# Attention of the first mixer: weighing by rounded and low parts instead of fp32 products, and one product for the two squares

## The reference

```python
proj = u @ w_in[l]
qk_raw, v, o_pre, gates, glu = jnp.split(proj, ...)
qk = jax.nn.silu(causal_dwconv(qk_raw, qk_conv_w[l], qk_conv_b[l]))
h = mlstm_chunkwise(heads(q), heads(k), heads(v), gates_i, gates_f)
h = rms_norm(h, ml_norm_g[l]) * jax.nn.sigmoid(o_pre)
y = causal_dwconv(a * jax.nn.sigmoid(gt), cv_dw_w[l], cv_dw_b[l])
y = jax.nn.silu(layer_norm(y, cv_ln_g[l], cv_ln_b[l]))
mix = jnp.concatenate([h, y], axis=-1) @ w_out[l]
```

## Time and profile before

| | us |
|---|---|
| median of 3 runs | 2322.71 |
| lowest and highest | 2318.79, 2326.07 |
| the profiled execution | 2319.68 |
| its span | 2317.9 |
| PE busy | 2218.1 (96%) |
| DVE busy | 1135.3 (49%) |
| ACT busy | 641.2 (28%) |
| POOL busy | 1481.5 (64%) |

### The profile page before, as it was taken

One profiled execution on the slowest core, in us unless ns is written; L12 is line 12 of the kernel. 1 busy time (PEld: TensorE's weight loads), 2 busy tenths in 40 slices (PEclk: granted clock), 3 DMA queues, 4 the chain that ended last, 5 costly groups with the idle time before them and its releaser, 6 DMA issues.

```text
span 2317.9 us, 27215 instructions
## 1 busy us (share of the span) xinstructions
PE 2218.1 (96%) x9696; PEld 1737.0 (75%) x9696; DVE 1135.3 (49%) x1971; ACT 641.2 (28%) x1108; POOL 1481.5 (64%) x710
## 2 busy tenths in 40 slices
PE   7999999999999998899999999997999989999997
PEld 4777776767888886788777888885777767888886
DVE  5778878884343104666543222006777844222101
ACT  2222323322222103444342111003555534111100
POOL 3756654566777887454278777887232238877785
PEclk9999999999999999999999999998999999999999
DMA  5322323642233332222123323331212212223232
GB/s 224 101 79 83 93 82 100 231 151 91 90 96 94 100 100 90 65 73 74 46 73 104 95 90 98 102 100 64 64 55 65 63 55 82 91 90 99 91 108 83
DMA packets 56513, 216.48 MB, mean 93 GB/s; under 512 B 6232, under 2 KB 6232, under 8 KB 53232
## 3 DMA queue, kind: packets, MB, share of 16 engines
q1 hardware_dynamic: 52992, 206.96, 27.6%
q10 hardware_dynamic: 3440, 8.44, 1.1%
HBM read 213.23 MB, written 2.15 MB: 93 GB/s over the span
## 4 chain that ended last, share of the span: by engine, by line
PE 56%; issue 22%; POOL 16%; DVE 4%; ACT 2%; POOLq 0%
PE ps L336 51%; POOL w_hi L868 8%; POOL w_lo L874 8%; PE ps L538 2%; ACT u_hi L420 1%; DVE u_lo L468 1%; DVE ps L485 1%; PE ps L1201 1%; PE ps L1233 1%; POOL acc L459 0%; PE ps L1208 0%; DVE ps L479 0%; PE ps L1247 0%; PE ps L375 0%; DVE ho L2190 0%
## 5 line engine op out<-in xcount | busy, mean ns | idle before, releaser
L868 POOL TENSOR_TENSOR w_hi<-raw,ones 128x1024 fp32r<-128x1024 f32 x315 | 602.0, 1911 | 595.3 <-DMA raw<-in_wstream 594.7
L874 POOL TENSOR_TENSOR w_lo<-raw,w_hi 128x1024 fp32r<-128x1024 f32 x342 | 837.7, 2449 | 194.6 <-ACT w_hi L1602 169.9
L336 PE MATMUL ps<-u_hi,w_hi 128*128 128x512 f32 x1760 | 719.0, 409 | 11.1 <-POOL w_lo L874 5.6
L336 PE MATMUL ps<-u_lo,w_hi 128*128 128x512 f32 x1760 | 698.5, 397 | 0.0
L336 PE MATMUL ps<-u_hi,w_lo 128*128 128x512 f32 x1760 | 698.0, 397 | 0.0
L336 PEld LDWEIGHTS ps<-u_hi,w_hi 128*128 128x128 f32 x1760 | 333.5, 190 | 89.5 <-issue 7.7
L336 PEld LDWEIGHTS ps<-u_hi,w_lo 128*128 128x128 f32 x1760 | 332.1, 189 | 81.6
L336 PEld LDWEIGHTS ps<-u_lo,w_hi 128*128 128x128 f32 x1760 | 333.2, 189 | 75.9 <-issue 3.1
L336 PE MATMUL ps<-f_hi,w_hi 128*128 128x512 f32 x528 | 208.6, 395 | 0.0
L336 PE MATMUL ps<-f_lo,w_hi 128*128 128x512 f32 x528 | 208.6, 395 | 0.0
L336 PE MATMUL ps<-f_hi,w_lo 128*128 128x512 f32 x528 | 208.6, 395 | 0.0
(11 more groups left out here) (328 smaller groups left out, 2894.8 us busy)
## 6 DMA issues: line engine op xcount, KB each, us to landing
raw<-in_wstream SPq DMA_DIRECT2D x342, 512.0 KB, 3.5
ada_buf<-in_ada SPq DMA_DIRECT2D x16, 1024.0 KB, 6.8
ada_start<-in_ada SPq DMA_DIRECT2D x8, 1024.0 KB, 16.7
cbc<-decay_rows ACTq DMA_DIRECT2D x8, 512.0 KB, 3.6
x<-in_xT SPq DMA_DIRECT2D x1, 2048.0 KB, 8.0
bc<-gate_rows ACTq DMA_DIRECT2D x4, 512.0 KB, 5.0
out_T<-x ACTq DMA_DIRECT2D x8, 256.0 KB, 2.2
prm<-in_params SPq DMA_DIRECT2D x1, 357.5 KB, 2.9
```

The lines of the kernel that those rows point to most:

```text
L336: last = nc.tensor.matmul(out, a, b, start=(start and k == 0 and i == 0), stop=(stop and k == nk - 1 and i == 2))
L868: g.tensor_tensor(w_hi[slot][:], raw[slot][:], ones[:, 0:1].to_broadcast([P, D]), ALU.mult).then_inc(chunk_hi, 1)
L874: g.tensor_tensor(w_lo[slot][:], raw[slot][:], w_hi[slot][:].bitcast(f32), ALU.subtract).then_inc(chunk_split, 1)
```

## The change

- The turned values and the product of scores and decays are held as a rounded part (`vt_hi`, `sp_hi`) and a low part (`vt_lo`, `sp_lo`). The numerators are three float32r products per block, the denominator two, with a float32r tile of ones (`ones_r`), which POOL fills at the start.
- ACT writes `vt_hi` where it wrote `vt`, and rounds `sp` (`att_high_act`: at the top of the next head, ahead of its first gate sigmoid; behind the last head ahead of the rounded heads). DVE forms `vt_lo` from banks 6 and 7 (`att_values_low_dve`, steps vl0, vl1, at the top of the next head ahead of the scores' product) and `sp_lo` (`att_low_dve`, step spl, behind it).
- PE waits in the scores for vl0 and vl1 instead of ACT's copies, and ahead of the denominator for spl instead of sp3.
- `vt_lo` lies on `vf`, `sp_hi` on `wt`, `sp_lo` on `sp`. So ACT writes `vf` and `wt` of the next head only when the numerators are done (num1).
- DVE adds the two squared numerators (`att_sum_dve`, step sum; after ten taps of the next head, and behind the divisor for the last one), and PE multiplies the sum with ones once.

```diff
@@ places
-    vt = place("vt", 2 * T, shape=[2, NT, P])
+    vt_lo = nc.alloc_sbuf_tensor_at("vt_lo", [P, 2, NT, P], f32r, offset=v_at)
+    vt_hi = place("vt_hi", 2 * T, f32r, [2, NT, P])
+    sp_hi = nc.alloc_sbuf_tensor_at("sp_hi", [P, 1280], f32r, offset=wt_at)
+    sp_lo = nc.alloc_sbuf_tensor_at("sp_lo", [P, 1280], f32r, offset=here[0])
@@ GpSimd
+        g.memset(ones_r[:].bitcast(f32), 1.0).then_inc(const_ready, 1)
@@ PE
                 if st in (1, 2):
-                    pe.wait_ge(a_v.sem, a_v.at(f"vt{st - 1}", h))
+                    pe.wait_ge(v_att.sem, v_att.at(f"vl{st - 1}", h))
...
-            pe.wait_ge(v_att.sem, v_att.at(f"sp{NT - 1}", h))
+            pe.wait_ge(v_att.sem, v_att.at("spl", h))
             for st in range(NT):
-                last = nc.tensor.matmul(ps[b][:, st * P:T], ones[:] if w is None else vt[:, w, st, :],
-                                        sp[:, WOFF[st]:WOFF[st] + T - st * P], start=(st == 0), stop=(st == NT - 1))
+                hi, lo = [t[:, WOFF[st]:WOFF[st] + T - st * P] for t in (sp_hi, sp_lo)]
+                if w is None:
+                    pairs = [(ones_r[:], hi), (ones_r[:], lo)]
+                else:
+                    pairs = tri(vt_hi[:, w, st, :], vt_lo[:, w, st, :], hi, lo)
+                last = matmuls(ps[b][:, st * P:T], pairs, start=(st == 0), stop=(st == NT - 1))
...
-            pe.wait_ge(v_att.sem, v_att.at("dn", h))
-            for e in range(2):
-                pe.wait_ge(a_n.sem, a_n.at(f"n{e}", h))
-                last = nc.tensor.matmul(ps[3][:], ones[:], sq[e][:], start=(e == 0), stop=(e == 1))
-            p_att.did(last, "hs")
+            pe.wait_ge(v_att.sem, v_att.at("sum", h))
+            p_att.did(nc.tensor.matmul(ps[3][:], ones[:], sq[0][:], start=True, stop=True), "hs")
@@ ACT
             if h:
-                act.wait_ge(v_att.sem, v_att.at(f"sp{NT - 1}", h - 1))
+                act.wait_ge(p_att.sem, p_att.at("num1", h - 1))
...
+        def att_high_act(h):
+            act.wait_ge(v_att.sem, v_att.at(f"sp{NT - 1}", h))
+            a_n.did(A(sp_hi[:], sp[:], ACT.Identity), "sph")
...
         for h in range(H1):
+            if h:
+                att_high_act(h - 1)
             gate_act(h, 0)
...
                 if h and e == 0:
-                    act.wait_ge(p_att.sem, p_att.at("vt1", h - 1))
+                    act.wait_ge(p_att.sem, p_att.at("num1", h - 1))
...
+        att_high_act(H1 - 1)
         act.wait_ge(gemm_done, C_WOUT1)
@@ DVE
+        def att_values_low_dve(h):
+            for e in range(2):
+                dve.wait_ge(a_v.sem, a_v.at(f"vt{e}", h))
+                v_att.did(V.tensor_tensor(vt_lo[:, e, :, :], ps[6 + e][:].rearrange("p (s c) -> p s c", c=P),
+                                          vt_hi[:, e, :, :].bitcast(f32), ALU.subtract), f"vl{e}")
...
+        def att_low_dve(h):
+            dve.wait_ge(a_n.sem, a_n.at("sph", h))
+            v_att.did(V.tensor_tensor(sp_lo[:], sp[:], sp_hi[:].bitcast(f32), ALU.subtract), "spl")
+        def att_sum_dve(h):
+            dve.wait_ge(a_n.sem, a_n.at("n1", h))
+            v_att.did(V.tensor_tensor(sq[0][:], sq[0][:], sq[1][:], ALU.add), "sum")
...
             if h:
+                att_values_low_dve(h - 1)
                 att_scores_dve(h - 1)
+                att_low_dve(h - 1)
                 att_divisor_dve(h - 1)
             gated(h, 0)
-            conv_taps(h, 0, 29, 16)
+            conv_taps(h, 0, 29, 20)
+            if h:
+                att_sum_dve(h - 1)
+            conv_taps(h, 0, 19, 16)
...
+        att_values_low_dve(H1 - 1)
         dve.wait_ge(p_ln.sem, p_ln.at("mu"))
         for n in range(KT):
             v_ln.did(V.tensor_tensor(y[:, n, :], y[:, n, :], ps[4][:], ALU.subtract), f"yc{n}")
         att_scores_dve(H1 - 1)
+        att_low_dve(H1 - 1)
...
         att_divisor_dve(H1 - 1)
+        att_sum_dve(H1 - 1)
         att_variance_dve(H1 - 1)
```

More of the change, by code:

```diff
@@ L126, in build @@
     ones = place("ones", P)
+    ones_r = place("ones_r", P, f32r)
     mean_w = place("mean_w", P)
@@ L701, in build @@
     v_dg = Steps(ctx, nc, "diag_dve", ["diag"])
-    v_att = Steps(ctx, nc, "att_dve", [f"sp{i}" for i in range(NT)] + ["dm", "dn", "d2", "vr", "h0", "h1", "hg0", "hg1"])
+    v_att = Steps(ctx, nc, "att_dve", ["vl0", "vl1"] + [f"sp{i}" for i in range(NT)] + ["spl", "dm", "dn", "d2", "sum", "vr", "h0", "h1", "hg0", "hg1"])
     a_sg = Steps(ctx, nc, "gate_sig_act", ["sg0", "sg1"])
@@ L709, in build @@
     a_wt = Steps(ctx, nc, "decay_act", [f"dg{i}" for i in range(NT)] + [f"off{i}" for i in range(NT - 1)])
-    a_n = Steps(ctx, nc, "att_act", ["n0", "n1", "ln", "rstd"])
+    a_n = Steps(ctx, nc, "att_act", ["sph", "n0", "n1", "ln", "rstd"])
     p_att = Steps(ctx, nc, "att_pe", ["vt0", "vt1", "qk0", "qk1", "qk2", "qk3", "den", "num0", "num1", "hs"])
@@ L849, in _ @@
         g.memset(eps_col[:, 1:2], 1e-37).then_inc(const_ready, 1)
-        pool.wait_ge(const_ready, 9)
+        pool.wait_ge(const_ready, 10)
         for t in (ident, ident_b):
@@ L909, in _ @@
     def _(pe):
-        pe.wait_ge(const_ready, 16)
+        pe.wait_ge(const_ready, 17)
         pe.wait_ge(v_set.sem, v_set.at("lv71"))
@@ L1294, in _ @@
         a_set.did(A(cvec[:], prm[:, COL["c"]:COL["c"] + KT], ACT.Sigmoid), "sig_c")
-        act.wait_ge(const_ready, 16)
+        act.wait_ge(const_ready, 17)
         norm_act(act, norms[0], None, lambda n: mod[:, n:n + 1])
@@ L1395, in _ @@
                         act.wait_ge(p_att.sem, p_att.at(f"vt{e_}", h))
-                        a_v.did(A(vt[:, e_, :, :], ps[6 + e_][:], ACT.Identity), f"vt{e_}")
+                        a_v.did(A(vt_hi[:, e_, :, :], ps[6 + e_][:], ACT.Identity), f"vt{e_}")
         for n in range(KT):
@@ L1676, in _ @@
         v_set.did(V.tensor_tensor(cvec[:], cvec[:], prm[:, COL["c"]:COL["c"] + KT], ALU.mult), "c")
-        dve.wait_ge(const_ready, 16)
+        dve.wait_ge(const_ready, 17)
         v_set.did(V.tensor_tensor(number[2], number[0], number[1], ALU.bitwise_xor), "xor")
```

## The result

| | before | after |
|---|---|---|
| median, us | 2321.32 (4 runs) | 2338.36 (4 runs, 2336.25 to 2344.44) |
| the profiled execution, us | 2319.68 | 2338.52 |
| its span, us | 2317.9 | 2336.7 |

The account below looks back on a forecast made before the run. It took PE as the bound, matmuls busy 96% of the span. Stalls 12.2 + clock 6.0 - products 6.0 + end 6.7 = +18.9 us, from 2319.68 to 2338.6, as a median 2341.6, range 2330 to 2352.

Parts of the forecast that it names:

- The stalls: PE waits in scores block 1 for DVE's vl0: 5.7, 3.1 and 3.4 us after heads 0 to 2, sum 12.2.
- The clock: PE's clock falls behind each stall, costing 2.0 us (0 to 2.9) each: +6.0 us for three stalls.
- The rival without a fall: PE's clock does not fall behind the stalls: +10.9 us, 2333.6; chance 0.17.
- The products: Fewer PE passes in numerators, denominator and squares: 2.0 us saved per head, 6.0 for three heads.
- The three heads together: Stalls 12.2, clock +6.0 and products -6.0 over the three heads between gemms: 12.2 us.
- The end of the stage: Behind the last head: stall 3.1, clock 2.0, rounding 1.2, d2 and sum 1.3, one product less 0.86: +6.7 us.
- Costs put at nothing: Between heads, rounding and low part of sp, sum of squares, moved reuse waits; at the start, the memset: hidden or free.
- the margin of 2.3 us: In each head, sp's chain takes 4.7 us after the scores; PE reaches the denominator after 7.0, so no wait.
- The contention rival: Low part of sp on DVE slowed beside POOL to 6.9 us, about 3.1 us per head: 2350.9; chance 0.10.
- The covered wait: DVE reads the banks before PE ends scores block 0, so no stall: -4.4 us, 2318.3; chance 0.08.

Follow-up runs that it names:

- The experiment with the wait alone: Kernel before, fp32 products unchanged, plus DVE's two subtractions at the change's place, results unused, with the scores waiting for them: 2344.74 us, ratio 1.0098.
- the first experiment: The changed kernel with DVE's low parts of the values moved before the last eight taps of the same head: 2322.11 us, ratio 1.0001.
- the reordering: The first experiment's kernel with another order of DVE's and ACT's steps behind the last head: 2321.68 us, ratio 0.9987 to the kernel before.
- the experiment with the later scores: The changed kernel with the scores four weight tiles later in PE's gemm, DVE's order untouched: 2329.64 us, ratio 1.0032 to the kernel before.
- the last experiment: The reordering's kernel without DVE's running sum of the last convolution tile; PE forms the mean in two products: 2314.55 us, ratio 0.9959 to the kernel before.
- the last two experiments: The reordering (2321.68 us) and the same kernel with the last running sum moved from DVE to PE (2314.55 us).

## Why the prediction was right

- **The stalls** came where and by what they were said to come. Behind the last head the release was forecast 6.7 us after the scores' start (378.91 - 372.20) and came at 6.9 (389.14 - 382.23). In the heads 12.2 us were forecast and 9.34 measured, and nearly all of the difference is in the first: 5.7 forecast, 3.10 found. There PE reached the scores 2.1 us later than before, held up by DVE already in the queries and keys (the 2.5 us for qk in the view of waits), while the release was at 139.77, forecast 140.10. That the release came so near is luck: DVE began its running sum 1.8 us later than before (138.42 against 136.66), but found POOL done and took 0.69 us for it instead of 2.77. That each head has its stall anew held: 3.14 and 3.10 against 3.1 and 3.4.
- **The clock.** 2.0 per stall was a mean of a widely spread quantity, and so it came by the windows: 3.3, 1.7 and 0, 5.0 in the three heads against 6.0. The experiment with the wait alone gave 1.00, 0.79 and 0.79 behind stalls of the same length. The rival without a fall (2333.6) is out, but single stalls did go without.
- **The products.** 6.0 forecast, 2.14 + 2.22 + 2.22 = 6.6 measured where nothing disturbs them: 0.86 a head for the squares, exactly as worked out, and 1.2 to 1.4 for the weighing against 1.15.
- **The three heads together**: 2.1 (later start) + 9.3 + 5.0 - 6.6 = 9.8; the last head's scores started 10.0 us later than before (382.23 against 372.20). Forecast: 12.2. The 2.1 are probably of the kind that the last section describes, and no effect of the change. The waiting came to 11.4 instead of 12.2 us, the clock to 5.0 instead of 6.0 and the saving to 6.6 instead of 6.0; all three missed in the same sense, the forecast too high by 2.2 us in all.
- **The end of the stage.** Forecast +6.7; measured 45.66 - 38.93 = +6.7. Two misses cancel in it. Up to the product of the mean the change lost 12.19 - 6.10 = 6.1 us against the scores' start, where stall and clock had been put at 3.1 + 2.0; behind it, to the first `y_lo`, only 33.47 - 32.83 = 0.6, where 1.6 had been forecast. The kernel before had a clock of 0.79 in the window from 380 us, and its eight products of the squares of y (L1030) took 9.18 us; in the change they took 7.70 at full clock. The additions without stall and clock, 1.2 + 1.3 - 0.86 = 1.6, are better read from the first experiment: +2.0. The two waits behind it, 1.6 for `sp_lo` and 2.2 for the sum, are what the reordering took away.
- **Costs put at nothing.** In the heads the denominator and the squares' product never waited, and the low part of sp took 1.49 us every time. But the margin of 2.3 us holds only while DVE is not held up before it. In the first experiment `sp_lo` was ready 0.10 and 0.18 us before the denominator in the first two heads (146.75 against 146.85, 225.07 against 225.25), since the running sum, held up behind POOL, ended 2.2 to 2.3 us after PE's scores (142.33 and 220.65) and `sp` came after it. The contention rival (2350.9) did not come, since POOL was idle there; that it would come beside a busy POOL is shown only for the running sum and not for this instruction. The rival's own sum has a slip: 9.9 against 7.0 is 2.9 us a head and not 3.1, which gives about 2350.4.
- **The covered wait** (2318.3) was the rival on the other side. The first experiment makes its condition true and gives 2322.11, so the mechanism was right and its price 4 us too good. In the profile the heads saved 0.6 more than forecast, the end took 2.0 instead of 1.6, the first scores started 2.9 us later, and the stages behind took 2.3 us longer; the last two are not the edit's.

So by the first `y_lo` the change had lost 16.8 us (427.89 against 411.13) where the steps gave 18.9, and the term that was mis-sized is the heads' 12.2, which measured 10.0. The profiled execution ended 18.8 us later only because 2 more us were lost in later stages. That the two agree to 0.1 us is chance; the medians' 17.0 is the better figure for the change. Where the 2 us came from was not tried.

## What to carry to other kernels

When a second engine begins to read a buffer, ask first where that engine is in its own program when the buffer is wanted: here two instructions of 0.6 us made a change without net effect 17 us slower, because DVE came to them 4 to 6 us after PE's scores had begun, and cost nothing once they stood eight taps earlier. A stop of the busiest engine can cost more than its own length, so price the clock behind it as a range. And when a reordering shows its waits gone but not its gain, look for the instruction that grew.

## What the runs showed of the hardware

**Instructions of DVE and POOL that both read two tensors from SBUF exclude each other.** Which of the two waits is decided by who starts first, be it by a tenth of a microsecond or less. The spread of L1753 in the earlier trace rows, 1.17 to 2.77 us for the same shape, is this. POOL in the kernel before, around the four of them:

```profile
136.48 2.40 POOL L874 TENSOR_TENSOR w_lo<-raw,w_hi 128x1024 fp32r<-128x1024 f32 x1
...
214.91 1.89 POOL L868 TENSOR_TENSOR w_hi<-raw,ones 128x1024 fp32r<-128x1024 f32 x1 [2.16 <-DMA raw<-in_wstream]
...
295.77 1.89 POOL L868 TENSOR_TENSOR w_hi<-raw,ones 128x1024 fp32r<-128x1024 f32 x1 [2.22 <-DMA raw<-in_wstream]
...
375.80 1.89 POOL L868 TENSOR_TENSOR w_hi<-raw,ones 128x1024 fp32r<-128x1024 f32 x1 [2.02 <-DMA raw<-in_wstream]
```

POOL ends at 138.88, 216.80, 297.66 and 377.69; the running sums, begun while it ran, end at 139.43, 217.34, 298.21 and 378.24, each 0.54 or 0.55 us later, however early they had begun. The change's sum at 386.76 (1.72 us) fits as well: POOL's instruction from 386.04 took 1.89 us, and 387.93 + 0.55 = 388.48. It holds the other way round too, and for `sp_lo`: in the experiment with the later scores `sp_lo` began 1.1 to 1.3 us before POOL in each head, still took 1.49 us, and POOL's instruction took 1.98 to 2.09 us instead of 1.89. The subtraction `vt_lo`, with one of its inputs in PSUM, is not held up: at 139.03 the two took 1.28 us together while POOL's instruction ran from 138.51 to 141.32. The Trainium skill (SBUF — State Buffer, SBUF: two separate sides) says that the shared pair of ports is an exclusive lock and that whichever starts first has it for the whole instruction. The trace agrees in each of these cases. The prediction had cited a milder rule, that such instructions contend, and had priced the rival of a slow `sp_lo` in proportion to its length (6.9 us). By the lock it would instead have been the rest of POOL's instruction and its own 1.49; with the 2.40 us of POOL's longer instruction (L874 above) that is an estimate of 3.9 us at most, and 1.69 + 1.31 + 3.9 = 6.9 is still inside the 7.0 us that PE gives.

**The same lock probably moves the start of the first scores.** In the gates' arithmetic a scan runs beside POOL's first rounding of weights. The kernel before, DVE and POOL:

```profile
68.56 1.19 DVE L1729 TENSOR_TENSOR_SCAN rm<-rlf,rz 4x512 f32<-4x512 f32 x1
...
68.64 2.80 POOL L868 TENSOR_TENSOR w_hi<-raw,ones 128x1024 fp32r<-128x1024 f32 x1 [20.86 <-DMA raw<-in_wstream]
```

The change:

```profile
68.86 2.84 DVE L1743 TENSOR_TENSOR_SCAN rm<-rlf,rz 4x512 f32<-4x512 f32 x1
...
68.54 2.08 POOL L873 TENSOR_TENSOR w_hi<-raw,ones 128x1024 fp32r<-128x1024 f32 x1 [20.79 <-DMA raw<-in_wstream]
```

DVE first: 1.19 us; DVE second: 2.84. DVE's first gating product then starts at 78.91 instead of 77.02, and PE waits 2.5 us for DVE at 113.37. That the one leads to the other is read from the timelines; no run tried it alone. It is not the only such place: in the last experiment the scan was the slow one too, but the running sum at 109.18 took 0.70 us (1.61 in the change), and PE waited 0.8 us at that point and began the scores at 133.22. So some two microseconds in this stage seem to hang on the order of two starts. That such a difference says nothing of an edit is shown: the last two experiments have the same instructions up to there, and their first scores start at 135.53 and 133.22.

**The clock behind a stop is not a function of its length.** Stops of 2.9 to 3.14 us were followed by windows of 0.59, 0.79, 1.00, 1.00, 0.79 and 0.79 in two kernels, and stops of 5.0 to 5.1 us by 0.64, 0.79 and 0.61. What decides it was not looked for.
